# Sigmoid gates of the merge by seven products in two of four k groups, and the forget gate's weight parts in one operand

## The reference

```python
h = rmsnorm(x, mix_norm[l])
proj = h @ w_in[l]
q_d, k_d, v_d, q_f, k_f, v_f, f_logit, g_d, g_f = jnp.split(proj, split_points, axis=-1)
...
log_f = jax.nn.log_sigmoid((f_logit + b_forget[l]).astype(jnp.float32))
...
merged = (jax.nn.sigmoid(g_d + b_gate_dil[l]) * (y_dil @ w_proj_dil[l])
          + jax.nn.sigmoid(g_f + b_gate_fox[l]) * (y_fox @ w_proj_fox[l]))
x = x + merged @ w_out[l]
```

## Time and profile before

| | |
|---|---|
| median of 3 runs | 2069.49 us (2069.41 to 2069.68) |
| the profiled execution | 2069.33 us |
| its span | 2067.4 us |
| PE (TensorE matmul) busy | 2053.4 us, 99% of the span, 9344 matmuls |
| PE weight loads busy | 1702.8 us, 82% |
| DVE busy | 1680.3 us, 81% |
| ACT busy | 1206.9 us, 58% |
| granted TensorE clock | 0.999 of full speed |
| weights moved | 195 GB/s over the span from memory |
| turns 1 to 3 of the merge | from 1080.9 us to about 1347 us of the span |

### The profile page before, as it was taken

One profiled execution on the slowest core, in us unless ns is written; L12 is line 12 of the kernel. 1 busy time (PEld: TensorE's weight loads), 2 busy tenths in 40 slices (PEclk: granted clock), 3 DMA queues, 4 the chain that ended last, 5 costly groups with the idle time before them and its releaser, 6 DMA issues.

```text
span 2067.4 us, 26644 instructions
## 1 busy us (share of the span) xinstructions
PE 2053.4 (99%) x9344; PEld 1702.8 (82%) x9344; DVE 1680.3 (81%) x1703; ACT 1206.9 (58%) x1394; POOL 87.6 (4%) x80
## 2 busy tenths in 40 slices
PE   9999999999999999999999999999999999999998
PEld 7788888888888888888888888888888888888886
DVE  7999999999999744555455655689999999999997
ACT  6666666666666444554544344466666666666664
POOL 0000000000000000000000000000000000000000
PEclk9999999999999999999999999999999999999999
DMA  8578777778877455545445665555877777887773
GB/s 280 204 220 256 231 236 247 233 217 250 238 234 242 141 195 186 183 163 174 162 156 197 198 202 194 184 185 181 251 237 232 246 231 224 244 243 231 246 232 126
DMA packets 222139, 441.01 MB, mean 213 GB/s; under 512 B 7648, under 2 KB 7824, under 8 KB 221936
## 3 DMA queue, kind: packets, MB, share of 16 engines
q1 hardware_dynamic: 202112, 401.64, 56.1%
q0 software_dynamic: 19744, 38.28, 11.2%
q10 hardware_dynamic: 208, 0.08, 0.0%
HBM read 400.13 MB, written 2.10 MB: 195 GB/s over the span
## 4 chain that ended last, share of the span: by engine, by line
PE 96%; DVE 2%; ACT 1%; issue 1%; DMA 0%; SPq 0%; ACTq 0%; DVEq 0%
PE ps L551 20%; PE ps L553 20%; PE ps L552 20%; PE ps L564 9%; PE ps L566 9%; PE ps L565 9%; PE ps L761 2%; PE ps L763 2%; PE ps L762 2%; PE ps L616 1%; DVE w_lo L1316 0%; DVE w_lo L1355 0%; DMA raw<-in_ffn_w_gate 0%; PE ps L772 0%; PE ps L597 0%
## 5 line engine op out<-in xcount | busy, mean ns | idle before, releaser
L1316 DVE TENSOR_TENSOR w_lo<-raw,w_hi 128x1024 fp32r<-128x1024 f32 x256 | 312.9, 1225 | 287.8 <-ACT w_hi L988 287.6
L988 ACT ACTIVATE w_hi<-raw 128x1024 fp32r<-128x1024 f32 x256 | 269.9, 1058 | 305.7 <-PE ps L553 301.0
L1355 DVE TENSOR_TENSOR w_lo<-raw,w_hi 128x1024 fp32r<-128x1024 f32 x280 | 338.0, 1219 | 7.2 <-ACT w_hi L1001 5.1
L551 PE MATMUL ps<-w_hi,xT_hi 128*128 128x512 f32 x856 | 340.0, 397 | 0.4 <-DVE xT_lo L1390 0.4
L553 PE MATMUL ps<-w_hi,xT_lo 128*128 128x512 f32 x856 | 334.1, 390 | 0.0
L552 PE MATMUL ps<-w_lo,xT_hi 128*128 128x512 f32 x856 | 333.6, 390 | 0.0
L1001 ACT ACTIVATE w_hi<-raw 128x1024 fp32r<-128x1024 f32 x280 | 290.8, 1053 | 72.5 <-PE ps L553 53.8
L1001 ACT ACTIVATE w_hi<-sums 128x1024 fp32r<-128x1024 f32 x160 | 169.8, 1063 | 203.7 <-PE ps L553 71.4
L1355 DVE TENSOR_TENSOR w_lo<-sums,w_hi 128x1024 fp32r<-128x1024 f32 x160 | 195.2, 1222 | 34.0 <-ACT w_hi L1001 31.4
L551 PE MATMUL ps<-w_hi,hT_hi 128*128 128x512 f32 x536 | 208.9, 390 | 0.0
L553 PE MATMUL ps<-w_hi,hT_lo 128*128 128x512 f32 x536 | 208.7, 389 | 0.0
(11 more groups left out here) (251 smaller groups left out, 3840.8 us busy)
## 6 DMA issues: line engine op xcount, KB each, us to landing
raw<-in_ffn_w_up SPq DMA_DIRECT2D x88, 1024.0 KB, 5.4
raw<-in_ffn_w_down SPq DMA_DIRECT2D x88, 1024.0 KB, 5.3
raw<-in_ffn_w_gate SPq DMA_DIRECT2D x87, 1024.0 KB, 5.4
raw<-in_w_in SPq DMA_DIRECT2D x80, 1024.0 KB, 5.0
xres<-gate_buf POOLq DMA_DIRECT2D x72, 512.0 KB, 5.5
raw<-in_w_out SPq DMA_DIRECT2D x16, 1024.0 KB, 5.1
raw<-in_w_proj_dil SPq DMA_DIRECT2D x8, 1024.0 KB, 5.1
raw<-in_w_proj_fox SPq DMA_DIRECT2D x8, 1024.0 KB, 5.1
```

The costliest lines, as they stand in the source:

```text
L551: nc.tensor.matmul(acc, hi, hi_w[:, j], start=first and j == 0, stop=False)
L988: nc.scalar.activation(slot_hi(place, offset), raw_half(place, offset), ACT.Copy).then_inc(hi_ready, 1)
L1316: nc.vector.tensor_tensor(slot_lo(place, offset), raw_half(place, offset), slot_hi(place, offset).bitcast(F32), ALU.subtract).then_inc(lo_ ...
L1355: nc.vector.tensor_tensor(slot_lo(place, offset), step_source(r)[0], slot_hi(place, offset).bitcast(F32), ALU.subtract).then_inc(lo_ready, 1)
```

## The change

In turns 1 to 3, k groups 0 and 2 of the two gates are done as seven products each (g_f takes the place of "up", g_d of "gate"), groups 1 and 3 directly. A turn has 38 slabs in place of 32: seven products (slabs 0 to 6), group 1 directly (7 to 10), seven products (11 to 17), group 3 directly (18 to 21), projections (22 to 29), down (30 to 37). The two transposes of `hidden` both go into bank 6 (T), which "up" uses from slab 9 on: token tile 0 ahead of slab 2, token tile 1 ahead of slab 7. The ring stays at four slabs. The token sums are made in turn 0 by DVE and ACT, into buffers that other parts have left. The forget gate's `f_hi` and `f_lo` become one stationary operand of 16 columns, so that a k tile takes two matmuls, and DVE adds the two halves of the result. The order of the ring in the second SwiGLU block shifts by two places, since the number of slabs ahead of it has changed.

```diff
+M_PAIR_AT, M_PAIR_GROUPS, M_PAIR_LOADS = (0, 11), (0, 2), ((0, 1), (4, 5))
+M_DIRECT_AT, M_DIRECT_GROUPS, M_DIRECT_LOADS = (7, 18), (1, 3), ((2, 3), (6, 7))
+M_PROJ_AT, M_DOWN_AT, MERGE_STEP, MERGE_LOADS = 22, 30, 38, 16
...
-                acc = ps[0:HEADS, B, 0:SEQ]
+                acc = ps[0:2 * HEADS, B, 0:SEQ]
                 pe.wait_ge(xt_lo, (NN + n + 1) * TT)
                 for k in range(n * CT, (n + 1) * CT):
-                    nc.tensor.matmul(acc, f_hi[:, k], xT_hi[:, k], start=k == 0, stop=False)
-                    nc.tensor.matmul(acc, f_lo[:, k], xT_hi[:, k], start=False, stop=False)
-                    done = nc.tensor.matmul(acc, f_hi[:, k], xT_lo[:, k], start=False, stop=k == KT - 1)
+                    nc.tensor.matmul(acc, f_both[:, k], xT_hi[:, k], start=k == 0, stop=False)
+                    done = nc.tensor.matmul(acc, f_both[:, k], xT_lo[:, k], start=False, stop=k == KT - 1)
...
+            def merge(q):                                   # PE
...
+                def seven(p):
+                    for o, (bank, lhs) in enumerate((
+                            (M7, of_pair(p, S3)), (M1, of_tile(p, 0, 0)), (M5, of_pair(p, S1)),
+                            (M6, of_pair(p, S2)), (UP0, of_pair(p, S4)), (GATE + 1, of_tile(p, 1, 1)),
+                            (GATE, of_tile(p, 1, 0)))):
+                        yield o
+                        product(place, M_PAIR_AT[p] + o, bank, lhs, p == 0, p == 1 and bank < GATE)
...
+                pe.wait_ge(gated, used + 2 * TT)
+                pe.wait_ge(merge_combined, q * M_COMBINED)
+                pe.wait_ge(merge_s_lo, 1)
+                for o in seven(0):
+                    if o == 2:
+                        transpose_tokens(hid, 0, T)
+                    if o == 5:
+                        pe.wait_ge(added, base)
+                pe.wait_ge(ht_lo, hid + 1)
+                transpose_tokens(hid, 1, T)
+                gate_directly(0)
+                pe.wait_ge(ht_lo, hid + TT)
+                up_directly(0)
+                pe.wait_ge(merge_s_lo, M_PAIRS)
+                for o in seven(1):
+                    pass
+                gate_directly(1)
+                up_directly(1)
                 for g, banks in enumerate((A, B)):
...
+                    pe.wait_ge(merge_combined, q * M_COMBINED + (1, 3)[g])
...
+            def round_merge(q, offset):                     # ACT
...
+                act.wait_ge(slab_done, place.slab(offset - MIX_RING + 1))
+                nc.scalar.activation(slot_hi(place, offset), src, ACT.Copy).then_inc(hi_ready, 1)
...
+            def merge(q):
+                place, hid = merge_place(q), q * TT + HID["mix"]
                 for o in range(MERGE_STEP):
+                    round_merge(q, o + MIX_RING)
+                    if o in (3, 8):
+                        round_tokens(hid, o // 8, T)
+                    if o == 18:
+                        act.wait_ge(slab_done, place.slab(18))
+                        nc.scalar.activation(partial[:, PART_M1], ps[:, M1], ACT.Copy)\
+                          .then_inc(merge_m1_copied, 1)
+                    if o in (21, 23):
+                        g = o // 23
+                        sigmoids(g, (q + 1) * (2 * TT) + g * TT)
...
+                if e in (13, 17):                           # DVE, turn 0
+                    sum_merge_pairs((e - 13) // 4)
+                if e in (20, 22):
+                    split_merge_pairs((e - 20) // 2)
...
+            def merge(q):                                   # DVE
...
+                    split_merge(q, o + MIX_RING)
+                    if o in (3, 8):
+                        split_tokens(hid, o // 8, T)
...
+                    if o == M_PROJ_AT + HALF_W - 1:
+                        merge_projection(place, o + 1, 0, A, (q + 1) * (2 * TT) + TT)
```

More of the change, by code:

```diff
@@ L100, in step_slab, with merge_slab @@
     return "down", None, r - DOWN_AT
+def merge_slab(r):
+    for pair, first in enumerate(M_PAIR_AT):
+        if first <= r < first + PAIR_SLABS:
+            return "paired", pair, r - first
+    for d, first in enumerate(M_DIRECT_AT):
+        if first <= r < first + 4:
+            return "direct", d, r - first
+    return "rest", None, r - M_PROJ_AT
 C_ID, C_CUM, C_DIL, C_COS, C_SIN, C_TRI, C_END = 0, 128, 384, 768, 832, 896, 1024
@@ L140, in __init__ @@
         else:
[L141 removed]
+            self.origin, self.ring = FFN2_ORIGIN, FFN_RING
     def slab(self, offset):
@@ L301, in step_source, with merge_source @@
         return raw[:, l % LOADS, o % 2 * 2:o % 2 * 2 + 2, :], l
+    merge_sums = (merge_sum_0[:, :, :], merge_sum_1[:, :, :])
+    def merge_source(r):
+        kind, which, o = merge_slab(r)
+        if kind == "paired":
+            what, part = PRODUCTS[o]
+            if what == "sum":
+                return merge_sums[SUM_PLACE[part]], None
+            l = M_PAIR_LOADS[which][what == "gate"]
+            return raw[:, l % LOADS, part::2, :], l
+        l = M_DIRECT_LOADS[which][o // 2] if kind == "direct" else M_PROJ_AT // 2 - 3 + o // 2
+        return raw[:, l % LOADS, o % 2 * 2:o % 2 * 2 + 2, :], l
     ident = tab[:, C_ID:C_ID + P]
@@ L956, in merge @@
                         pass
                 pe.wait_ge(gated, used + (2 + 1) * TT)
-                down(place, MERGE_FIRST, hid, base, next_too=last)
+                pe.wait_ge(merge_combined, (q + 1) * M_COMBINED)
+                down(place, M_DOWN_AT, hid, base, next_too=last)
                 pe.wait_ge(added, base + NN - 1)
-            for i in range(NN - 2):
-                merge(mix_place(MERGE + MERGE_FIRST + i * MERGE_STEP), i, False)
-            merge(mix_place(MERGE_LAST - MERGE_STEP), NN - 2, True)
@@ L966, in _ @@
-            last_down(mix_place(MERGE_LAST), HID["mix"] + (NN - 1) * TT, ADDED["mix"] + (NN - 1) * NN, 2)
+            for q in range(MERGES):
+                merge(q)
+            last_down(last_merge, HID["mix"] + (NN - 1) * TT, ADDED["mix"] + (NN - 1) * NN, 2)
             ffn(1, 2)
@@ new lines, in merge_projection @@
+            def merge_projection(place, offset, g, banks, count):
+                dve.wait_ge(slab_done, place.slab(offset))
+                dve.wait_ge(gate_done, count)
+                for t in range(TT):
+                    gate = gate_buf[:, g, t if g == 0 else 1 - t]
+                    nc.vector.tensor_tensor(hidden[:, t] if g == 0 else gate, ps[:, banks + t], gate,
+                                            ALU.mult).then_inc(gated, 1)
+                if g == 1:
+                    dve.wait_ge(gated, count)
+                    for t in range(TT):
+                        nc.vector.tensor_tensor(hidden[:, t], hidden[:, t], gate_buf[:, 1, 1 - t], ALU.add)\
+                          .then_inc(hidden_ready, 1)
@@ L1769, in _ @@
+            for q in range(MERGES):
+                merge(q)
+            last_down(last_merge, first_place(1), 2, 1.0)
             ffn(1, 2)
```

289 lines of the change are left out of this document (227 added, 62 removed).

## The result

| | before | after |
|---|---|---|
| median | 2069.49 us (2069.41 to 2069.68) | 2081.61 us (2080.78 to 2084.72) |
| ratio | | 1.0061 [1.0048, 1.0075] |
| profiled execution, its span | 2069.33 us, 2067.4 us | 2081.66 us, 2079.9 us |
| granted TensorE clock | 0.999 | 0.995 |

What follows compares the result with a forecast made beforehand. PE, busy 99% of the span, was taken as the bound. Savings -8.16 and -0.91 plus waits +9.87, +3.96 and +0.3 gave +5.06 us on 2069.33 us: 2074.4 us, range 2071.5 to 2080.

Steps and rivals of the forecast that it cites:

- The matmuls saved: PE in the merge: products in place of direct groups, 36 fewer matmuls over three turns, 8.16 us saved.
- wait 3: Start of turns 2 and 3: PE waits for DVE's lo part at product 4, 0.15 us a turn, 0.3 us in all.
- Wait 1: Slab 9 of each of three turns: PE waits for DVE to take token tile 1 out, 3.29 us each, 9.87 us.
- Wait 2: Seam from turn 0 to turn 1: PE waits until DVE has multiplied both tiles of the second projection, 3.96 us.
- The forget gate: Forget chunks: third and fourth save 0.91 us; the first two give theirs back waiting for xT_lo ahead of the third.
- rival 1: Clock falls to half in the gaps of Wait 1 and Wait 2; 2076 to 2082 us, most likely 2078; chance 0.23.
- The price: Cost of one clock fall: PE may run slow for 3 to 4 us and lose 1 to 2 us.
- The rule cited from the Trainium skill: PE gaps above about 3 us halve the clock; at least Wait 2 would pay, giving 2076 us or more.
- It fits by 0.1 us: Turn 0, slab 20: last head's lo part ends at 1069.57, PE uses it at 1069.87; costed at nothing, up to 0.3.

Runs made afterwards that it cites:

- both edits: Experiment 3: changed kernel with token tile 1 two slabs earlier and the seam's products in other banks, second projection multiplied one lo part earlier; 2062.62 us, ratio 0.9967.
- experiment 12: Changed kernel with 12 matmuls of zeros ahead of each wait at slab 9, the waits kept; 2077.3 us.
- experiment 1: Changed kernel with token tile 1 rounded and split two slabs earlier; 2066.94 us, ratio to before 0.999.
- experiment 2: Changed kernel with the seam's first two products in banks 0 and 1 and DVE multiplying the second projection one lo part earlier; 2075.22 us, executions 2072.64 to 2078.65.
- experiment 6: Kernel before with the forget gate's part of the change alone, 32 matmuls in place of 48; 2068.53 us against 2069.44 us.
- experiment 4: Kernel with both edits, the two token sum additions of turn 0 behind slabs 11 and 13 instead of 13 and 17; 2063.52 us.
- experiment 10: Kernel of experiment 4 with the second token-sum pair's lo part moved behind the lo part of slab 5; 2063.86 us.
- experiment 8: Kernel with both edits, PE made to wait for four ACT copies ahead of slab 9 in turns 1 to 3, gaps of 2.75 us; 2073.25 us.
- experiment 7: Kernel with both edits, PE made to wait for two ACT copies ahead of slab 9 in turns 1 to 3, gaps of 1.43 us; 2067.75 us.

## Why the prediction missed

**The matmuls saved** were right. With both edits the step of a turn is 2.35 us shorter: from product 2 of turn 2 to product 2 of turn 3,

```profile
1170.52 0.47 PE L650 MATMUL ps<-w_hi,merge_hi 128*128 128x512 f32 x1
...
1256.10 0.48 PE L650 MATMUL ps<-w_hi,merge_hi 128*128 128x512 f32 x1
```

it takes 85.58 us; the kernel before needs 1191.24 - 1103.31 = 87.93 us for a turn:

```profile
1103.31 0.48 PE L551 MATMUL ps<-w_hi,xT_hi 128*128 128x512 f32 x1
...
1191.24 0.48 PE L551 MATMUL ps<-w_hi,xT_hi 128*128 128x512 f32 x1
```

The term says 2.72; wait 3 takes 0.24 of it back, and 0.13 us are not placed.

**Wait 1** was right: slab 9 starts at 1105.56 in place of 1102.33 (where the filling matmuls of experiment 12 start), 3.23 us; by the medians of experiments 12 and 1 it is (2077.3 - 2066.94) / 3 = 3.45, forecast 3.29. **Wait 2** was right: PE started at 1084.66, forecast 1084.64. That it agrees to 0.02 us is luck: DVE ended 0.15 us later than in the sum's 1084.46, and PE started 0.05 us behind it and not 0.18. **Wait 3** was right in kind: at product 4 of turns 2 and 3 of the kernel with both edits two starts in a row stand 0.35 and 0.34 us apart in place of 0.2267, together 0.24 us a turn, forecast 0.15. **The forget gate** had the forecast wait ahead of the third chunk, 0.68 us for xT_lo.

**The step that failed is the weight of rival 1.** The prediction saw that the clock had fallen 3.0 us behind the last matmul, and wrote: "Against it stands that three of the four gaps are not longer than the stretch that was just enough". It took one observation at the end of the kernel for a threshold and, finding the gaps at it, gave the falls 0.23; the sum puts them at nothing, and the range leaves out three or more. The runs show no threshold there: with gaps of 2.75 and 3.07 us the clock falls in some places and not in others, and in the changed kernel's profiled execution it fell at all four. The place that the 3.0 us came from is itself no fixed distance. Behind the last matmul of the kernel with the gaps of 1.43 us the clock fell after 2.4 us (2058.07 to about 2060.45), behind that of experiment 12 after 5.2 us (2067.21 to about 2072.4), and in the other traces after times between these:

```profile
2057.68 0.39 PE L757 MATMUL ps<-w_hi,last_lo 128*128 128x512 f32 x1
2060.00:2061.00 1.00, 0.00 (x0) 0.00 (x0) 0.81 (x4) 0.32 (x2) 0.00 (x0) 0.72 0.00 0
...
2066.82 0.39 PE L759 MATMUL ps<-w_hi,last_lo 128*128 128x512 f32 x1
2072.00:2073.00 1.00, 0.00 (x0) 0.00 (x0) 0.00 (x0) 0.00 (x0) 0.00 (x0) 0.68 1.05 375
```

The price, "lose 1 to 2 us", was right: 4.3 us for three falls by experiment 12, 4.8 by experiment 1 (14.67 less the forecast 9.87; 4.3 if the waits are taken as 3.45 each), so **1.4 to 1.6 us each**. At the seam the whole stretch fell on a working PE: 3.4 us hold 8 starts 0.427 us apart and 15 at 0.2267, 7 x 0.2267 = 1.6 us. The rule cited from the Trainium skill ("TensorE: Matmul & The Clock Gate", "Why this matters for your kernels"), no PE gap above about 3 us, pointed the right way, and gave "2076 or more". This case's traces agree for 3.07 us at five places of six (experiment 2 has the sixth), and show one fall at 2.75 us too.

**A second, smaller miss is in turn 0.** "It fits by 0.1 us" compared the last head's lo part with the time at which PE had wanted it *before*, without moving PE ahead by the 0.91 us that the same sum had just taken off. The lo part ended at 1069.12 + 0.42 = 1069.54 (forecast 1069.57), but PE came earlier and waited 0.48 us:

```profile
1069.12 0.42 DVE L1823 TENSOR_TENSOR yT_lo<-ps,yT_hi 128x256 fp32r<-128x256 f32 x1
```

At slab 20 PE was then 0.22 us ahead of before (1069.65 against 1069.87) and not 0.9, and the seam took the rest, since its end is DVE's. So the forget gate's 0.91 us, real by experiment 6, was worth nothing in the changed kernel. Experiments 4 and 10, two other orders, did not get it back: in them DVE works without a pause from the landing of a transfer (1071.5) to the fourth or fifth product.

**The books.** 2074.4 + 4.3 to 4.8 (three falls at slab 9, with what the waits cost beyond 9.87) + 1.6 (the seam) + 0.9 (the forget gate) = 2081.2 to 2081.7; measured 2081.61.

## What to carry to other kernels

Price a new gap on a full PE twice: its length, and the matmuls behind it at half speed. Here gaps of 0.35 and 1.43 us cost their length and some 0.3 us each, and gaps of up to 1.8 us left the clock at full in every trace. Gaps of 2.75 us brought it down at one place of three, of 3.07 us at five of six, and of 3.67 us and more at all seven that were traced, each time for some 1.5 us. If the wait cannot be moved, matmuls that add zeros get the fall back. When a step finishes earlier, ask what it arrives at: shift PE in the sum before comparing it with an operation of another engine. And look first at where an operation stands in the order: one number, 6 for 8, was worth 14.7 us here.

## What the runs showed of the hardware that was not expected

The clock's fall does not follow from the length of a gap alone: with the same 3.07 us idle it came at once, 1.5 us after PE was at work again, or not at all, in one execution (experiment 2). What decides that is not shown by these runs. A stretch at half speed inside the merge lasted about 3.4 us each time in the traces, also when it began 1.5 us after PE was at work again. Scatter is a sign of such gaps: three of 2.75 or 3.07 us spread the executions over 6 us (experiments 2 and 8), where the kernels with none above 1.9 us (experiments 3, 4, 6, 7, 10) agree within 0.5 to 1.5 us. It is a weak sign for one gap: experiments 1 and 12, with the seam's 3.7 us alone, agree within 1.5 us too.
